# Routing in a two-layer mixture of experts: token rows made by matmul, logits computed from streamed tokens, expert outputs scaled in the experts' own rows, and the join in two passes

## What is computed

```
x = layer_norm(ALPHA * x + g1 * o_x, ln1_g, ln1_b)          # the same for ctx in layer 0
hx = x * (1 + sc2) + sh2                                    # the tokens that the experts see
y = hier_moe(tokens, w_rg, b_rg, w_re, b_re, w1, w3, w2)
x = layer_norm(ALPHA * x + g2 * y, ln2_g, ln2_b)

def hier_moe(h, ...):
    g_logit = h @ w_rg + b_rg                               # 4 groups
    e_logit = (h @ w_re + b_re) of the best group           # 8 experts in it
    e_val, e_idx = top_k(e_logit, 2)
    gates = p_group * softmax(e_val)
    # the tokens are gathered by expert in units of rows, each unit runs
    #   (silu(xb @ w1[e]) * (xb @ w3[e])) @ w2[e]
    # and every token adds its two rows, each times its gate
```

## Time and profile before

| what | us |
|---|---|
| median of 3 runs | 3009.38 |
| lowest and highest | 3007.46, 3013.77 |
| the profiled execution | 3015.98 |
| its span in the trace | 3014.2 |

### The profile page before, as it was taken

The page is one execution under the profiler, slowest core; times in us unless marked ns, Lnnn a source line. Parts: engine busy times, 40 slices in busy tenths (PEclk is TensorE's granted clock), DMA queues, the critical chain, the costliest instruction groups (busy, mean ns, idle before and its releaser), DMA issues. The chain is left out here.

```text
span 3014.2 us, 45233 instructions
## 1 busy us (share of the span) xinstructions
PE 2576.2 (85%) x17001; PEld 1735.7 (58%) x17002; DVE 1321.2 (44%) x2487; ACT 618.1 (21%) x1310; POOL 626.2 (21%) x625
## 2 busy tenths in 40 slices
PE   7999989999999998989938999889488873798754
PEld 6877766488885574557525555445267661454432
DVE  6752367248999923347271111111434734222113
ACT  3540178120000011026110000000221620010002
POOL 3432012014540000311145100000122214321101
PEclk9999999999999999989958999999789976899876
DMA  3231320137555632030128889999531124999995
GB/s 142 91 126 61 137 78 26 62 101 232 208 190 222 247 119 70 1 143 5 50 97 348 326 352 421 405 409 384 217 125 73 75 105 199 373 373 381 403 420 202
DMA packets 139194, 602.55 MB, mean 200 GB/s; under 512 B 20544, under 2 KB 40924, under 8 KB 92096
## 3 DMA queue, kind: packets, MB, share of 16 engines
q1 hardware_dynamic: 88576, 367.18, 32.1%
q10 hardware_dynamic: 41808, 212.75, 17.6%
q0 software_dynamic: 8688, 21.00, 1.9%
HBM read 581.92 MB, written 33.75 MB: 204 GB/s over the span
## 5 line engine op out<-in xcount | busy, mean ns | idle before, releaser
L1440 DVE SCALAR_TENSOR_TENSOR psum<-weight_ring,condition_rows 128x1024 f32<-128x1024 f32 x192 | 268.0, 1396 | 16.0 <-issue 0.9
L3062 DVE COPY expert_hidden_turned<-psum 128x128 f32<-128x128 f32 (+1 forms) x93 | 32.7, 352 | 464.8 <-PE psum L2923 464.8
L268 PE MATMUL psum<-weight_ring 128*128 128x256 f32 (+1 forms) x896 | 222.2, 398 | 3.2 <-POOL weight_ring L253 3.2
L2912 PE MATMUL psum<-weight_ring,residual 128*32 128x256 f32 x2176 | 146.5, 415 | 75.8 <-DMA weight_ring<-in_w_dram 44.4
L2901 PE MATMUL psum<-weight_ring,residual 128*64 128x256 f32 x1792 | 206.1, 383 | 0.7 <-issue 0.7
L268 PEld LDWEIGHTS psum<-weight_ring 128*128 128x128 f32 x896 | 170.8, 191 | 43.4 <-issue 4.5
L251 POOL TENSOR_TENSOR weight_ring<-weight_ring 128x512 f32<-128x512 f32 x31 | 42.7, 1377 | 622.2 <-ACT keys L1883 382.0
L2901 PEld LDWEIGHTS psum<-weight_ring,residual 128*64 128x64 f32 x1792 | 127.4, 138 | 77.0 <-issue 17.6
L2930 PE MATMUL psum<-weight_ring,expert_hidden_turned 128*32 128x256 f32 (+1 forms) x1536 | 165.8, 441 | 0.0
L174 PE MATMUL psum<-ffn_hidden,weight_ring 128*128 128x512 f32 (+1 forms) x440 | 154.5, 514 | 4.1 <-DVE ffn_hidden L1485 4.1
L2901 PE MATMUL psum<-third_stream_weights,residual 128*64 128x256 f32 x896 | 120.0, 428 | 35.1 <-DMA third_stream_weights<-in_w_dram 35.1
(11 more groups left out here) (519 smaller groups left out, 4615.0 us busy)
## 6 DMA issues: line engine op xcount, KB each, us to landing
third_stream_weights<-in_w_dram ACTq DMA_DIRECT2D x93, 2048.0 KB, 17.1
weight_ring<-in_w_dram SPq DMA_DIRECT2D x84, 2048.0 KB, 17.4
weight_ring<-in_w_ada_dram SPq DMA_DIRECT2D x24, 2048.0 KB, 8.9
weight_ring<-in_w_ffn_dram SPq DMA_DIRECT2D x11, 2048.0 KB, 12.5
weight_ring<-in_w_rnn_dram SPq DMA_DIRECT2D x8, 1536.0 KB, 6.5
weight_ring<-in_w_att_dram SPq DMA_DIRECT2D x6, 2048.0 KB, 8.0
weight_ring<-in_w_in_dram SPq DMA_DIRECT2D x6, 2048.0 KB, 8.8
weight_ring<-in_w_down_dram SPq DMA_DIRECT2D x8, 1408.0 KB, 6.1
```

Of the source, the lines that this page charges most:

```text
L268: last = c.nc.tensor.matmul(to, weights[:, k * P:(k + 1) * P], rhs[:, k], start=(starts and k == 0), stop=(stops and k == KH - 1), skip_gr ...
L1440: last = v.scalar_tensor_tensor(out=product, in0=w[:, t], scalar=1.0, in1=CR[:, n, :], op0=ALU.mult, op1=ALU.mult, accum_out=c.mod[:, i // ...
L2912: last = nc.tensor.matmul(ps[units.rows(2 * m + o), 2 + b, 0:256], XT[:, b, k % tiles, units.rows(k // tiles)], w[:, k, 256 * o:256 * (o + ...
L3062: v.tensor_copy(HT[:, b, :, :], ps[:, 1, 0:256].rearrange("p (k s) -> p k s", k=2)[:, :, 0:2 * cap])\
```

## The change

It has these parts, in the order of the program.

1. `mixer_project` feeds the ring two chunks less; those two loads are issued in `layer_norm`, behind the router's constants.
2. The router no longer loads the modulation rows spread over 128 partitions. It loads scale and shift rows into two partitions. `route` no longer loads the residual's rows at its start.
3. The logits: TensorE holds 64 scaled weight columns (36 and 28 zeros) and streams 512 or 256 tokens past them, even and odd eighths of the width in the two halves of the partitions. ScalarE copies the result, TensorE turns it back by tiles, and VectorE adds the two halves. The means and roots of all tokens are turned into two rows too.
4. GpSimd builds, in `layer_norm`, 8 diagonal matrices of 128x128 for each of sequence and context, the identity times the scale. In `route` the token rows of a tile come from TensorE: for each half of 512 columns one product with the two rows (mean, root) against (scale, shift), and four products of 128x128 with the diagonals. ScalarE copies them out, times the token's inverse root, and SyncE stores them. GpSimd only clears the gather rows and issues the gathers.
5. In `experts`, VectorE takes the result out of PSUM times g2 (`weigh`); in layer 0 it first forms each unit's g2 rows from those of sequence and context. ScalarE only issues the stores. The residual is worked in two halves: one before GpSimd's loop of gathers, one behind it, for which ScalarE loads gain and bias after its own loop.
6. The join has two passes of VectorE a tile, XR plus row times gate, straight from the gathered rows. ScalarE has the copies of the sequence's columns. SyncE feeds the ring at once, beside the gathers.
7. `route` and `experts` end without the drain of GpSimd, and the block of `mean_weights` is gone.

```diff
@@ layer_norm
+                def logits(v):
+                    at, n = pieces[v]
+                    for k in range(KT):
+                        h = slice(64 * (k % 2), 64 * (k % 2) + 64)
+                        last = nc.tensor.matmul(ps[h, logit_bank(v), 0:n], WS[:, k, v, 0:64], X[:, k, at:at + n],
+                                                start=(k < 2), stop=(k >= KT - 2))
+                    last.then_inc(logits_ready.sem, 1)
@@ Router.load
-        sp.dma_start(self.MOD[:, :, :].rearrange("p r n -> p (r n)"),
-                     self.c.row_table[self.l:self.l + 1, 0:4 * D].partition_broadcast(P)).then_inc(self.rows_in.sem, 16)
+        for n, row in enumerate((SCALE_ROW, SHIFT_ROW)):
+            sp.dma_start(self.AFFINE[n:n + 1, :, :].rearrange("p v n -> p (v n)"),
+                         self.c.row_table[self.l:self.l + 1, row * D:(row + self.nv) * D]).then_inc(self.consts.sem, 16)
@@ route, TensorE
+                def rows(t):
+                    v, tok = 0 if t < ST else 1, slice(t * P, (t + 1) * P)
+                    if t >= 2:
+                        router.made.wait(pe, t - 1)
+                    for h in range(2):
+                        bank = 2 * (t % 2) + h
+                        nc.tensor.matmul(ps[:, bank, :], router.MROWS[0:2, tok], router.AFFINE[0:2, v, h * 512:(h + 1) * 512],
+                                         start=True, stop=False, skip_group_check=True)
+                        for k in range(KH):
+                            last = nc.tensor.matmul(ps[:, bank, k * P:(k + 1) * P], c.X[:, KH * h + k, tok],
+                                                    router.DIAG[:, v, KH * h + k, :], start=False, stop=(k == KH - 1),
+                                                    skip_group_check=True)
+                    last.then_inc(router.ready.sem, 1)
@@ experts, GpSimd
-                for t in range(nt):
-                    for h in range(2):
-                        x = XR(t)[:, h * D // 2:(h + 1) * D // 2]
-                        nc.gpsimd.tensor_tensor(x, x, R.affine[h], ALU.mult)
-                        pool.drain()
-                        nc.gpsimd.tensor_tensor(x, x, R.affine[2 + h], ALU.add)
+                residual(0)
                 with pool.Fori(1, last) as it:
                     for b in range(NSTREAM):
                         gather(it, b)
+                residual(1)
+                pool.drain()
@@ experts, ScalarE
                 def store(n, b, it):
-                    y_out[b].wait(act, it * (16 * groups))
-                    nc.scalar.copy(YS[:, b, :], ps[:, 5 + b, 0:cols]).then_inc(y_copied.sem, 1)
                     y_copied.wait(act, n + 1)
@@ experts, VectorE
+                def weigh(it, b):
+                    n = it * NSTREAM + b
+                    y_out[b].wait(dve, it * (16 * groups))
+                    if not quarters:
+                        v.tensor_copy(NOW[:, b:b + 1], CTX[:, bass.ds(n, 1)])
+                        dve.drain()
+                        v.scalar_tensor_tensor(out=YS[:, b, :], in0=R.gates[1], scalar=NOW[:, b:b + 1], in1=R.gates[0],
+                                               op0=ALU.mult, op1=ALU.add)
+                        dve.drain()
+                    y_done.wait(dve, n + 1)
+                    v.tensor_tensor(YS[:, b, :], ps[:, 5 + b, 0:cols], R.gates[0] if quarters else YS[:, b, :], ALU.mult)\
+                        .then_inc(y_copied.sem, 1)
@@ combine_and_norm
-                rows_in[nt - 1].wait(sp, 32)
                 ring.feed(sp, ring.uses + Ring.SLOTS)
+                def add(k, i):
+                    return v.scalar_tensor_tensor(out=XR(i), in0=choice(k, i), scalar=R.gate[:, k, i:i + 1], in1=XR(i),
+                                                  op0=ALU.mult, op1=ALU.add)
```

327 lines of the change are left out of this document (196 added, 131 removed).

## The result

The changed kernel takes 2979.6 us, the median of four runs (2976.22 to 2983.59), against 3010.04 for the kernel before in the same session (3007.46 to 3013.77). The ratio is 0.9898 with a 95% interval of 0.9881 to 0.9916. So it is faster, by 30 us in the medians or 1.0%. The forecast was 66 us less, 2943.6, with a range that ended at 2972.

A forecast was written before the change was run, and what follows sets the result against it. The prediction took the work itself to bound the experts and chains of short steps on one engine to bound the six small stages; its terms summed to 65.8 us, 3009.4 - 65.8 = 2943.6 us, range 2923 to 2972.

The forecast's parts named there:

- The price of a tile: Routing: three tiles of token rows ahead of the rank products take TensorE 13.9 us, near the full clock.
- a PEclk of 0.5 through the row products: Routing: sign that the forecast is wrong, TensorE staying at 1.2 GHz through the token rows.
- the 0.5 of the block: Removing the block of `mean_weights` gives 0.5 us.
- The counts: Routings: counts begin 15.7 and 15.1 us into the stage, gaining 15.7 us in layer 0 and 8.4 in layer 1.
- fit before the table's products: Routing: the other three tiles, 12 us, fit before the table's products, 14.6 us behind the counts.
- half clock: Rival: TensorE stays at 1.2 GHz through token rows, 22 us lost plus 4 in layer norms, 2970 us; chance 0.14.
- tail of GpSimd: Rival: gain and bias land 5 us later, both experts stages end 5 and 4 us late, 2952 us; chance 0.06.
- The drain: End of both routings: leaving out GpSimd's drain gives 2.3 and 2.0 us.
- Experts: Experts: -0.3 us for VectorE's work, 5 gained by halving the residual, -1 at layer 0's end.
- the rival on the slower side: Experts: `weigh` comes onto the path of every unit, price 83 us, 3026 us; chance 0.04.
- Layer norms and joins: Layer norms gain 4 and 9 us, joins 11.5 and 8.7, in layers 0 and 1.
- The condition that the logits' products in the two halves of the partitions run side by side: Layer norm: 8 products of 512 cost 3.4 us side by side at full clock, 6.8 one after the other.

The follow-up runs named there:

- full rows: Changed kernel with the two-row products run over all 128 rows, the other 126 zero: 2943.76 us, ratio 0.9768.
- all together: Changed kernel plus full rows, two tiles ahead of rank products, exponentials earlier, next mixer's weights behind gathers, gain and bias loaded by GpSimd: 2927.24 us, ratio 0.9722.

## Why the prediction was wrong

Left out of this, because the change didn't make it, are 4.7 us by which the profiled span began better. Then 35.1 us are to be held against 65.8.

**The price of a tile, the step that failed.** The prediction took 13.9 us for three tiles, "near the full clock, since a stretch that began at half clock reached it in layer 0's layer norm". It measured 23.9. The prices themselves were near: 3.95 us at full clock was forecast and 3.5 is what full rows show, because four products of 128 columns cost 0.89 us, by their columns; 7.2 at half clock was forecast and 8.0 measured. The 7.2 holds for full rows: their first half tile, at a granted clock of 0.50, took 3.55 us, 7.1 a tile. Why a tile with two-row products takes 8.0 at the same granted clock stays open. The choice between the two levels was wrong, and the prediction had named its sign, a PEclk of 0.5 through the row products. The choice was drawn from products with all 128 rows in use and put on a stretch in which half of the columns come from products with two. The runs show that this is the difference: with these products filled with zeros to 128 rows the clock rises, with them left out it rises, and dense values in the other products change nothing. With full rows the kernel takes 2943.76 us, and every stage lies within 3.2 us of the forecast. That this is the forecast's 2943.6 to 0.2 us is luck: the routings came out 3.2 and 2.9 us shorter than forecast, the mixer and the experts of layer 1 2.4 and 3.1 longer, and 4.2 us more than the 0.5 of the block were gained ahead of the first changed stage.

The Trainium skill, TensorE: Matmul & The Clock Gate, Part 1 (the HAM clock gate), has the clock depend on how busy TensorE has been. By that rule 46.5 us without a gap would be at the full clock and the routings 37 and 36 us long, as with full rows; the trace disagrees (23.87 us busy of 23.87, granted clock 0.50), and the measurement decides.

**What hung on it.** The counts begin at 25.4 and 25.1 us instead of 15.7 and 15.1. In layer 0 that is 6.0 us gained instead of 15.7, in layer 1 1.6 us lost instead of 8.4 gained. Behind the counts the other tiles were held to "fit before the table's products"; in layer 0 they hold them by 4.8 us, and then the last store holds the gathers by 1.3. The rival *half clock* had this mechanism, with counts at 24 and 23.5 us and 6 us at the table, and 2970 us; it was given 0.14. Even it was 10 us short, though 4 us of its loss lay in the layer norms and did not come: it had nothing for the price of 8.0 instead of 7.2, for the late gathers and for the tail of GpSimd below.

**The drain.** 4.3 us were forecast; the run on the kernel before shows 7.0. In the changed kernel layer 1 got its 3.1. In layer 0 2.6 came, and the second set of gathered rows took 3.1 back. What delays it can be narrowed down by the gathers of all runs, issue to landing. In the changed kernel the second gather of layer 0 took 8.0 us, and ScalarE's weights for the third stream were issued 0.47 us behind it. The same stands in the two other runs in which the gathers were late, the one with the rank products behind one tile and the one with dense values (7.35 and 7.05 us, weights 0.35 and 0.47 us behind). In all other runs on the changed kernel these weights came 1.4 us or more behind the second gather, which took 2.8 us, and 0.4 us or less behind the third, which took over 7. The loads of gain, bias and g2 rows, issued 1 to 4 us ahead, are at most a part of it: in the version with all together they too landed up to 2.6 us behind the first gather's issue (3.9 in the changed kernel), and the second gather took 2.8 us. So the late gathers seem to have run into the next stage's weights, which the drain had held back; no run moves these weights alone, so this is read from the traces and not shown.

**Experts.** Forecast: -0.3, +5 and -1. The stall of the earlier trace rows is gone, and putting it back costs 13.8 us with the load in it. The late gathers of the start cost 3.1. The stage of layer 0 is 2.1 us shorter though it lost 3.1 at its start and 2.7 at its end, which leaves some 8 us for the stall and what followed it, where 5 were forecast. The *tail of GpSimd* is more than was forecast: 3.4 us lay between the last result and the next stage before, 6.1 and 7.2 lie there now, 2.7 and 3.7 us lost instead of 1 and 0. In layer 1 the prediction had GpSimd end at about 2968 of the old time, before the stage; it ended 0.3 us before the stage's end and set it. `weigh` costs nothing that can be seen: no row shows TensorE waiting for a result's buffer, and VectorE's 91 us more in the two experts stages (135.28 and 115.24 against 64.57 and 95.25) lie under the products, so the rival on the slower side had no support.

**Layer norms and joins.** Layer norms 28.8 and 20.7 against 28.6 and 21.3, joins 47.5 and 36.5 against 47.1 and 35.9. The condition that the logits' products in the two halves of the partitions run side by side held: the 8 of 256 columns took 1.9 us at full clock, where the price of the earlier trace rows makes 3.5 one after the other. In the join of layer 0 the first add came at 12.0 us instead of 10, and the steps behind it took 35.5 us instead of 37.

The Trainium skill, DMA: Bandwidth & Descriptors, section Queues, rings and completion order, spoke against feeding beside the gathers (each DMA engine serves its queues in turn). The trace agrees: without the weights beside them the first gathered rows come 4.5 us earlier and the join is 5.8 us shorter, where the prediction had 2.5 for it.

The mixer of layer 1 took 1.7 us more and, in other versions, 0.1 to 2.9 more than before (0.9 more in the kernel before without the drain); nothing in it was changed but the time of its loads, and no run separates that.

## What to carry to other kernels

When small work moves onto an idle TensorE, price it at both clock levels, and ask of a stretch at full clock whether its products use the array as the new ones will: products with a few rows of a long contraction are cheap in flops and dear for the clock, and filling them up with zeros was worth 36 us here. Look for every queue that the new work stands in: here its order on TensorE held the ranks, and its order on ScalarE held two exponentials that the same counts needed. And weights that the next stage doesn't wait for should not run beside gathers that this stage waits for. That holds for a drain that is left out too: here it let the next stage's weights start beside the last gathers.

## What the runs showed of the hardware

TensorE can be busy without a pause for 46.5 us and be granted 1.2 GHz for all but 4.6 us of it, when half of its columns come from products that use two of the 128 rows. The same columns with 128 rows, 126 of them zero, bring 2.4 GHz after half a tile (3.55 us), and the time of a tile falls from 8.0 to 3.5 us. The values that are streamed had no part in it (23.87 us for three tiles with a diagonal and with dense data). GpSimd's work with two SBUF inputs made VectorE's small steps 2.7 times as long on the mean in a place where nothing else was changed (0.51 against 0.19 us), by making 14 of 38 of them 0.8 to 1.3 us long. In layer 0 a gather of token rows took 6.9 to 8.5 us where ScalarE's loads of 2 MB were issued ahead of it or up to 0.5 us behind it, and 2.8 to 4.2 us where they came 1.4 us or more behind.
